# A recurrence's key norms taken by tokens and spread back by products, with new orders on three engines

## The reference

```python
kk = heads(k * p['k_k'])
kk = kk / jnp.maximum(jnp.sqrt(jnp.sum(kk * kk, axis=-1, keepdims=True)), 1e-12)
k = k * (1 + (a - 1) * p['k_a'])
decay = jnp.exp(-jnp.exp(heads(w)))
def step(S, inp):                      # b_t = kk_t * a_t
    sa = jnp.einsum('bhvk,bhk->bhv', S, kk_t)
    S = S * d_t[:, :, None, :] - sa[..., None] * b_t[:, :, None, :] + v_t[..., None] * k_t[:, :, None, :]
    return S, jnp.einsum('bhvk,bhk->bhv', S, r_t)
yn = ((y - mean) * lax.rsqrt(var + GN_EPS)).reshape(B, T, D) * p['lnx_g'] + p['lnx_b']
bonus = jnp.sum(heads(r * k * p['r_k']), -1, keepdims=True) * heads(v)
out = ((yn + bonus.reshape(B, T, D)).astype(h.dtype) * g) @ p['wo']
```

## Time and profile before

| | us |
|---|---|
| median of three timed runs | 3330.76 |
| the three runs | 3322.47, 3330.76, 3331.25 |
| the profiled execution | 3320.69 |
| its span in the trace | 3319.1 |
| TensorE busy, share of the span | 96% |
| VectorE busy, share of the span | 64% |
| ScalarE busy, share of the span | 42% |

### The profile page before, as it was taken

One profiled execution on the slowest core, in us unless ns is written; L12 is line 12 of the kernel. 1 busy time (PEld: TensorE's weight loads), 2 busy tenths in 40 slices (PEclk: granted clock), 3 DMA queues, 4 the chain that ended last, 5 costly groups with the idle time before them and its releaser, 6 DMA issues. The chain is left out here.

```text
span 3319.1 us, 80335 instructions
## 1 busy us (share of the span) xinstructions
PE 3188.2 (96%) x31492; PEld 2974.0 (90%) x31492; DVE 2127.6 (64%) x3654; ACT 1387.5 (42%) x2180; POOL 128.7 (4%) x245
## 2 busy tenths in 40 slices
PE   6999997888899999999999999999999999999998
PEld 3799986666799999999999988998999999999998
DVE  4544547778558778778778875555578855444455
ACT  2333325566345324334334564334455334343342
POOL 0000000000000000000000000000000000000000
PEclk9999999999999999999999999999999999999999
DMA  9877740000777888878867532342356754544443
GB/s 397 308 270 283 286 169 20 19 18 19 263 297 276 304 304 294 312 289 302 310 225 242 188 125 96 124 153 91 124 197 218 254 184 162 163 163 165 164 163 118
DMA packets 182917, 668.77 MB, mean 201 GB/s; under 512 B 21366, under 2 KB 21536, under 8 KB 182208
## 3 DMA queue, kind: packets, MB, share of 16 engines
q1 hardware_dynamic: 155808, 570.48, 48.2%
q0 software_dynamic: 26912, 95.47, 8.7%
HBM read 661.78 MB, written 4.09 MB: 201 GB/s over the span
## 5 line engine op out<-in xcount | busy, mean ns | idle before, releaser
L1127 DVE TENSOR_TENSOR sb_wlo<-sb_raw,sb_whi 128x1024 fp32r<-128x1024 f32 x778 | 942.8, 1222 | 523.5 <-ACT sb_whi L706 521.6
L706 ACT ACTIVATE sb_whi<-sb_raw 128x1024 fp32r<-128x1024 f32 x778 | 811.8, 1057 | 1107.9 <-PE ps L1941 1001.7
L1939 PE MATMUL ps<-sb_ah,sb_whi 128*128 128x288 f32 x3728 | 1111.1, 298 | 11.4 <-DVE sb_al L1333 6.9
L1940 PE MATMUL ps<-sb_ah,sb_wlo 128*128 128x288 f32 x3728 | 1099.7, 295 | 0.0
L1941 PE MATMUL ps<-sb_al,sb_whi 128*128 128x288 f32 x3728 | 1096.2, 294 | 0.0
L1939 PEld LDWEIGHTS ps<-sb_ah,sb_whi 128*128 128x128 f32 x3728 | 698.4, 187 | 38.5 <-issue 33.8
L1941 PEld LDWEIGHTS ps<-sb_al,sb_whi 128*128 128x128 f32 x3728 | 702.0, 188 | 0.0
L1940 PEld LDWEIGHTS ps<-sb_ah,sb_wlo 128*128 128x128 f32 x3728 | 699.9, 188 | 0.1
L1939 PE MATMUL ps<-sb_bh,sb_whi 128*128 128x288 f32 x2048 | 607.4, 297 | 0.0
L1940 PE MATMUL ps<-sb_bh,sb_wlo 128*128 128x288 f32 x2048 | 604.1, 295 | 0.0
L1941 PE MATMUL ps<-sb_bl,sb_whi 128*128 128x288 f32 x2048 | 602.2, 294 | 0.0
(11 more groups left out here) (307 smaller groups left out, 3346.0 us busy)
## 6 DMA issues: line engine op xcount, KB each, us to landing
sb_raw<-stream SPq DMA_DIRECT2D x1070, 512.0 KB, 4.5
sb_strip<-strips POOLq DMA_DIRECT2D x156, 512.0 KB, 5.0
sb_crow<-crow POOLq DMA_DIRECT2D x8, 512.0 KB, 5.4
sb_x<-xT SPq DMA_DIRECT2D x1, 2304.0 KB, 15.6
sb_x<-xT POOLq DMA_DIRECT2D x1, 2304.0 KB, 9.3
yT<-sb_x SPq DMA_DIRECT2D x4, 576.0 KB, 2.8
sb_lwa<-lw POOLq DMA_DIRECT2D x16, 130.0 KB, 2.3
sb_lwg<-lw POOLq DMA_DIRECT2D x16, 130.0 KB, 2.4
```

The source lines that it names most:

```text
L706: nc.scalar.activation(whi[:, q % SPL, :], raw[:, n, :], ACT.Copy).then_inc(hi_ready, 1)
L1127: nc.vector.tensor_tensor(wlo[:, q % SPL, :], raw[:, n, :], whi[:, q % SPL, :], ALU.subtract).then_inc(lo_ready, 1)
L1939: mm(out, wh, xh, start=start, stop=False)
L1940: mm(out, wl, xh, start=False, stop=False)
```

## The change

The vectors k_k and k_a are put at the end of the table `vec` (32 more columns) and leave the lane's weights; the three scalars made of them (k_k squared, minus k_k, 1 - k_a) are computed once for all 16 pairs ahead of the stage (`prm`, 3 x 16 columns), and `gain` keeps only its wait for the free lane. `ssq` is ten products of one column, which put the sum of squares of each token in a partition; `floor` and `norm` work on 5 columns (`kn`); a new `spread` on TensorE multiplies the inverses, broadcast along a row, with the identity, so that 320 columns lie in PSUM again, and `removal` reads them there behind a new wait. `normed` subtracts and scales with two operations over 320 columns in place of five tensor-scalars. `gated` is cut in `output` (the addition) and `gated` (the product with the gate), and TensorE's `grams` in `gram_b` and `gram_k`. The lists of the three engines are put in a new order; the places within a turn are to be seen in the diff. Semaphore counts follow.

```diff
@@ -61,7 +61,9 @@
...
-NVEC = QG + 4
+KKG = QG + 4
+KAG = KKG + KB
+NVEC = KAG + KB
...
@@ -73,16 +75,16 @@
...
-PW0, PA0, PKK, PKA = range(2 * P, 2 * P + 4)
+PW0, PA0 = range(2 * P, 2 * P + 2)
...
-Z, SSQ, NAT, GK, GB = range(1, 6)
+Z, SSQ, SPR, NAT, GB, GK = range(1, 7)
...
-BONUS, GATE, BACK = range(1, 4)
-PRE, INVY, INVT, TOKM, POST, MSK, CHN = 5, 5, 6, 5, 3, 2, 4
+BONUS, BACK, GATE = range(1, 4)
+PRE, INVY, INVT, TOKM, POST, MSK, CHN = 6, 5, 6, 5, 3, 2, 4
...
@@ -92,7 +94,7 @@
...
-FRONT_CHAIN, BACK_CHAIN = 8, 15
+FRONT_CHAIN, BACK_CHAIN = 5, 12
...
@@ -303,6 +305,7 @@
...
+        prm = sb("prm", [P, 3, KB], "SMALL", 736)
...
@@ -328,7 +331,7 @@
...
-                                + [("st", [P, 2, C]), ("bn", [P, NCH, 6]), ("ag", [P, NCH, 2]), ("rs", [P, 8]), ("prm", [P, 3])]):
+                                + [("st", [P, 2, C]), ("bn", [P, NCH, 6]), ("ag", [P, NCH, 2]), ("rs", [P, 8]), ("kn", [P, 8])]):
...
@@ -836,9 +839,8 @@
             def gains(u, it):
...
-                act.wait_ge(m["omk"], it + 1)
-                nc.scalar.activation(t["t5"][:], t["sa"][:], ACT.Identity, scale=t["lwa"][:, PKA:PKA + 1],
-                                     bias=t["prm"][:, 0:1]).then_inc(m["t5"], 1)
+                nc.scalar.activation(t["t5"][:], t["sa"][:], ACT.Identity, scale=vec[:, bass.ds(2 * it + (KAG + u), 1)],
+                                     bias=prm[:, 0, bass.ds(2 * it + u, 1)]).then_inc(m["t5"], 1)
...
@@ -892,37 +894,39 @@
                 t = lanes[0 if f is None else f]
                 if f is not None:
                     sigmoids(f, i)
-                    gains(f, i)
-                    token(f, i, T_V, t["vt"][:], "ps")
                 if g is not None:
                     products(g, j)
                 if f is not None:
+                    token(f, i, T_V, t["vt"][:], "ps")
                     decay(f, i, 0)
+                    gains(f, i)
+                if g is not None:
+                    state(g, j, 0, CH_0)
+                if f is not None:
                     decay(f, i, 1)
                 if g is not None:
-                    state(g, j, 0, CH_0)
                     state(g, j, 1, CH_14)
+                if f is not None:
+                    token(f, i, T_KK, t["km"][:, :, 0, :], "ps")
+                if g is not None:
                     state(g, j, 2, CH_2)
                     state(g, j, 3, CH_3)
                     state(g, j, 4, CH_3)
-                if f is not None:
-                    token(f, i, T_KK, t["km"][:, :, 0, :], "ps")
-                if g is not None:
                     root(g, j)
                 if f is not None:
                     inverse(f, i, 1)
+                    inverse(f, i, 2)
                     token(f, i, T_MV, t["km"][:, :, 1, :])
-                    inverse(f, i, 2)
+                if g is not None:
+                    back(g, j)
+                if f is not None:
                     inverse(f, i, 3)
                     token(f, i, T_B, t["ng"][:, :, 0, :])
                 if g is not None:
-                    back(g, j)
-                if f is not None:
-                    token(f, i, T_K, t["kt"][:])
-                    inverse(f, i, 4)
-                if g is not None:
                     high(g, j)
                 if f is not None:
+                    inverse(f, i, 4)
+                    token(f, i, T_K, t["kt"][:])
                     inverse(f, i, 5)
...
             def turn(it):
@@ -1444,6 +1448,10 @@
...
+            kk = vec[:, KKG:KKG + KB]
+            ch.inc(nc.vector.tensor_tensor(prm[:, 2, :], kk, kk, ALU.mult))
+            ch.inc(nc.vector.tensor_scalar(prm[:, 1, :], kk, -1.0, None, ALU.mult))
+            ch.inc(nc.vector.tensor_scalar(prm[:, 0, :], vec[:, KAG:KAG + KB], -1.0, 1.0, ALU.mult, ALU.add))
...
@@ -1470,27 +1478,22 @@
             def gain(u, it):
...
-                dve.wait_ge(m["lwa"], 16 * it + 16)
-                kk = t["lwa"][:, PKK:PKK + 1]
-                ch.inc(tt(t["prm"][:, 2:3], kk, kk, ALU.mult))
-                ch.inc(nc.vector.tensor_scalar(t["prm"][:, 1:2], kk, -1.0, None, ALU.mult))
-                nc.vector.tensor_scalar(t["prm"][:, 0:1], t["lwa"][:, PKA:PKA + 1], -1.0, 1.0, ALU.mult, ALU.add).then_inc(m["omk"], 1)
...
             def squares(u, it):
...
-                stt(out=t["n2"][:], in0=kb, scalar=t["prm"][:, 2:3], in1=kb, op0=ALU.mult, op1=ALU.mult).then_inc(m["sq"], 1)
+                stt(out=t["n2"][:], in0=kb, scalar=prm[:, 2, bass.ds(2 * it + u, 1)], in1=kb, op0=ALU.mult, op1=ALU.mult).then_inc(m["sq"], 1)
...
             def floor(u, it):
...
-                ch.inc(nc.vector.tensor_scalar(t["n2"][:], t["ps"][:, Z_K:Z_K + TT], 1e-24, None, ALU.max))
+                ch.inc(nc.vector.tensor_scalar(t["kn"][:, 0:NCH], t["ps"][:, Z_K:Z_K + NCH], 1e-24, None, ALU.max))
...
             def norm(u, it):
...
-                ch.inc(nc.vector.reciprocal(t["n2"][:], t["n2"][:]))
+                nc.vector.reciprocal(t["kn"][:, 0:NCH], t["kn"][:, 0:NCH]).then_inc(m["sq"], 1)
...
@@ -1502,28 +1505,29 @@
...
-                be, kk = flat(t["bE"][:]), t["lwa"][:, PKK:PKK + 1]
+                be, kk = flat(t["bE"][:]), vec[:, bass.ds(2 * it + (KKG + u), 1)]
...
+            def erased(u, it):
+                t, m = lanes[u], L[u]
+                kb = flat(k[:, bass.ds(2 * it + u, 1), :])
+                dve.wait_ge(m["ex"], 2 * it + 1)
+                stt(out=t["kr"][:, :, 0, :], in0=chunks(kb), scalar=prm[:, 1, bass.ds(2 * it + u, 1)], in1=t["e"][:, :, 0:C],
+                    op0=ALU.mult, op1=ALU.mult).then_inc(m["prep"], 1)
+
             def received(u, it):
...
-                dve.wait_ge(m["ex"], 2 * it + 1)
...
-            def erased(u, it):
-                t, m = lanes[u], L[u]
-                kb = flat(k[:, bass.ds(2 * it + u, 1), :])
-                stt(out=t["kr"][:, :, 0, :], in0=chunks(kb), scalar=t["prm"][:, 1:2], in1=t["e"][:, :, 0:C],
-                    op0=ALU.mult, op1=ALU.mult).then_inc(m["prep"], 1)
-
             def removal(u, it):
...
+                dve.wait_ge(m["pre_mm"], PRE * it + SPR)
...
-                ch.inc(tt(be, be, t["n2"][:], ALU.mult))
+                ch.inc(tt(be, be, t["ps"][:, Z_K:Z_K + TT], ALU.mult))
...
@@ -1598,24 +1602,24 @@
...
-                for c in range(NCH):
-                    ins = nc.vector.tensor_scalar(t["yn"][:, c, :], t["ps"][:, Z_Y + C * c:Z_Y + C * c + C], t["ag"][:, c, 0:1],
-                                                  t["rs"][:, c:c + 1], ALU.subtract, ALU.mult)
-                    if c < NCH - 1:
-                        ch.inc(ins)
-                    else:
-                        ins.then_inc(m["yn"], 1)
+                ch.inc(tt(t["yn"][:], chunks(t["ps"][:, Z_Y:Z_Y + TT]), t["ag"][:, :, 0:1].to_broadcast([P, NCH, C]), ALU.subtract))
+                ch.wait()
+                tt(t["yn"][:], t["yn"][:], t["rs"][:, 0:NCH].rearrange("p (c t) -> p c t", t=1).to_broadcast([P, NCH, C]),
+                   ALU.mult).then_inc(m["yn"], 1)
...
             def bonus(u, it):
...
-            def gated(u, it):
+            def output(u, it):
...
+
+            def gated(u, it):
+                t, m = lanes[u], L[u]
...
@@ -1636,37 +1640,36 @@
                     squares(f, i)
                 if g is not None:
                     level(g, j, 5)
-                    bonus_in(g, j)
+                    solved(g, j)
                 if f is not None:
                     floor(f, i)
                 if g is not None:
-                    solved(g, j)
+                    products(g, j)
                 if f is not None:
+                    removed(f, i)
+                    running(f, i)
                     norm(f, i)
                 if g is not None:
-                    products(g, j)
-                if f is not None:
-                    running(f, i)
-                    removed(f, i)
-                if g is not None:
+                    bonus_in(g, j)
                     carries(g, j)
                 if f is not None:
+                    erased(f, i)
                     received(f, i)
-                    erased(f, i)
                     removal(f, i)
                     insertion(f, i)
+                    level(f, i, 0)
                 if g is not None:
                     moments(g, j)
                 if f is not None:
-                    level(f, i, 0)
                     grams(f, i)
                     level(f, i, 1)
                 if g is not None:
-                    bonus(g, j)
+                    normed(g, j)
                 if f is not None:
                     level(f, i, 2)
                 if g is not None:
-                    normed(g, j)
+                    bonus(g, j)
+                    output(g, j)
                 if f is not None:
                     level(f, i, 3)
                 if g is not None:
@@ -2127,20 +2130,32 @@
...
             def ssq(u, it):
...
-                pe.wait_ge(m["sq"], it + 1)
```

(66 more changed lines are left out.)

2 lines of the change are left out of this document (1 added, 1 removed).

## The result

The changed kernel takes 3290.61 us (median of four runs, 3289.40 to 3291.39), the kernel before on the same chip 3326.61 us (3320.52 to 3331.25): ratio 0.9896, 95% interval 0.9883 to 0.9909, a gain of 36 us where 43 were forecast. The span of the profiled execution went from 3319.1 to 3287.9 us, 31.2 less. The difference of the two gaps lies in the kernel before: its runs spread over 11 us and the profiled one is at their lower end, while those of the changed kernel lie within 2 us. (A ratio here is estimated from all runs of a group and is not quite the quotient of the two medians; both lie in the interval.) Further runs of the changed kernel gave 3290.23 and 3289.84 us (ratio 0.9897 both times), beside 3328.54 and 3323.78 us for the kernel before.

A forecast was written before the change was run, and what follows sets the result against it. Bound: a chain passing between engines, repeated each turn of the recurrence. 1.65 + 0.1 + 0.9 = 2.67 us a turn (3.07 behind the loop's jump) gave 43 us: 3320.7 to 3278, median 3283, range 3264 to 3312.

The forecast's parts named there:

- the 5 us that were added for the distance between profiled execution and median: Expected median 3283 us, 5 us above the profiled execution's forecast of 3278 us.
- Part 1: Turn's start to the carries: reciprocal off the path, carries at 4.1 instead of 5.76, gain 1.65 us (1.2 to 1.8).
- Rival (a): New orders worth nothing, only the reciprocal leaves the path: 16 us gained, 3305 to 3315 us; chance 0.22.
- Part 2: Carries to level 0, with the new spread: 7.7 instead of 7.84, gain 0.1 us (0.4 to a loss of 0.8).
- slack of the round trip: Between carries and level 0: small reciprocal done at 5.2, sums before the spread at 6.5, 1.3 us of slack.
- Part 3: Level 0 to the next turn: 7.66 instead of 8.57, gain 0.9 us (0.2 to 1.4).
- After the stage everything moves up as it is: Behind the recurrence: later work only starts earlier, as hardly any transfers run in the stage; no size given.
- (b): The norm's round trip between engines replaces the reciprocal on the path: no change, 3321 to 3331 us; chance 0.07.
- (c): Granted clock falls in the recurrence: slower from about 3 low turns on, 3355 us at 5; chance 0.07 with other slowing.
- (d): Spread hides wholly and TensorE's waits shrink more: 3.6 us in a turn, 3260 to 3266 us; chance 0.04.

The follow-up runs named there:

- orders alone: Changed kernel with the old norm over 320 columns (wide reciprocal, no spread), new orders, scalars and two-operation scaling kept: 3318.91 us, ratio 0.9984.
- norm alone: Kernel before with the new norm by tokens (narrow reciprocal, spread), its orders, lane scalars and five tensor-scalars kept: 3309.50 us, ratio 0.9954.
- tokens-v ahead: Changed kernel with tokens-v ahead of the products again in TensorE's and ScalarE's queues: 3296.77 us, ratio 0.9922.
- late norm: Changed kernel with the small reciprocal moved behind bonus-in, two additions and the erased keys in VectorE's queue: 3295.88 us, ratio 0.9919.
- old tail: Changed kernel with the order of before from level 1 on, on all three engines, two-operation scaling kept: 3304.64 us, ratio 0.9935.
- five tensor-scalars: Changed kernel with five tensor-scalars back in place of the two operations over 320 columns: 3295.08 us, ratio 0.9912.
- fetch moved: Changed kernel with the load of the next low-rank weights issued at a turn's start instead of 11 us into it: 3291.24 us, ratio 0.9889.

## Why the prediction was right, and what it missed

The time was hit more closely than the gain. In the trace 43 us were forecast and 31.2 came; of the 5 us that were added for the distance between profiled execution and median 1.2 came (3290.61 against 3289.40). The one error covers a third of the other, and that is luck.

**Part 1** (5.76 to 4.1): 4.14, and the time is right, but the cause only in part. The orders alone bring the carries to 4.17, with the wide reciprocal moved behind the copy; the norm alone brings them to 4.72, and with tokens-v ahead the changed kernel has 4.71. So the early carries come from the order, and what the narrow reciprocal is needed for lies in part 2: kept wide, it stands ahead of the gains, and level 0 comes 1.9 us later. Rival (a), in which the reciprocal by itself gave 1.65 here, gets 1.04.

**Part 2** (7.84 to 7.7): 7.71. The slack of the round trip was 1.27 us against 1.3, and the late norm shows that it isn't more. The spread is hidden better than forecast: 0.3 of its 0.58 were to be hidden, and the norm alone shows 0.07 paid. TensorE needs 2.96 us from the carries to state 1 before and 3.05 now, for the recall and the wait for ScalarE's scaled copy that stood there are gone. The removal starts 0.21 behind state 1, which follows the spread, and about 0.1 later than its queue would let it.

**Part 3** (8.57 to 7.66): 7.89, so 0.68 us where 0.9 were forecast. By the old tail and the five tensor-scalars the order gives about 0.4 of it and the two wide operations 0.24 of their 0.35.

**The mis-sized term** is this part, and it stands in the part's end. Up to level 2 the layout was right within 0.05 us; then gate (15.80 against 15.7) and level 3 (17.37 against 17.2) slip by 0.1 to 0.2, and from level 4 to the next turn there are 0.85 us (690.28 to 691.13) where I had 0.7, although show 1.01 for the same step (686.23 to 687.24). A turn of 19.70 instead of 19.5 is 15 x 0.2 = 3 us. The new groups cost 0.61 (sums of squares) and 0.68 us (spread), a little over the 0.58 that I took from one distance of the earlier trace rows. The Trainium skill (TensorEngine Tiling, Instruction Overhead) has one column cost what some sixty do: the trace agrees, 0.61 us for ten products of one column, and 0.58 to 0.68 for ten of 64 columns.

**The missing term** is the stops. Fifteen undisturbed turns would have given 15 x (22.33 - 19.70) = 39.5 us, 3.5 less than forecast; the stops and the clock (with the 0.8 of the jump) took 8.3 - 3.1 = 5.2 of it back in the fourteen full turns and 0.9 more went in the fifteenth. With 0.1 in the filling turn, 0.9 in the drain and 1.2 elsewhere (0.3 were forecast) this is the way from 43 to 31.2. That the waits of 1.6 and 1.2 us in each turn of the kernel before covered most of such stops is argued from their absence there; no run shows it by itself. In the drain I had put nothing: back waits for VectorE, and the gate behind it runs at half the clock. TensorE of the changed kernel in the drain:

```profile
825.45 0.90 PE L2098 MATMUL ps<-sb_con,sb_yt 64*64 64x64 f32 x20 [1.69 <-DVE sb_yt L1607]
826.27 1.33 PE L2268 MATMUL ps<-sb_mids,sb_lwg 128*128 128x288 f32 x2
```

The gate's two products take 1.33 us instead of 0.75 behind that wait, and the granted clock of the stretch is 0.83 where it was 0.91. "After the stage everything moves up as it is" held but for the 1.2 us; that the drain would be as before, which the sum took without saying it, did not.

**The rivals.** (a) falls by the old tail and tokens-v, together 1.5 us in a turn. (b) is real and 1.3 us away. (c) didn't decide: one turn in fifteen of the changed kernel has a clock of 0.93, and the kernel before has two. But its mechanism is in the orders alone, where every second turn falls to 0.92, and it is cheaper than the 14 us a turn that I priced, because the clock is low for a part of the turn only: about 0.85 us there, 1.5 and 1.8 in the two low turns of the kernel before, 3.9 in the one of the norm alone. Two figures of (c) were wrong from the start. By its own terms five low turns lose 5 x 14 and the ten others gain 10 x 2.9, so the kernel would be 41 us slower, not 27; and the earlier trace rows leave 8.6 us of idle time in 50, that is 3.8 us in a turn of 22.2, not 6, with 18.3 us of work and not 16.8. (d) had both the hidden spread and shorter waits; the spread does hide nearly whole, but the turn is 19.70 us, where (d) wanted 18.6.

## What to carry over

A chain that passes between engines and repeats is best priced by laying one turn out, queue by queue, with the durations of the trace, from meeting place to meeting place; that hit the carries and level 0 here within 0.05 us and the turn within 0.2, while the busy shares said nothing. A second thing can be late close behind the first: a change that removes one of them alone gives little (14 and 5 us here) and must not be judged before both are gone (36 us). A time that comes out right does not show its cause: the early carries were put down to the reciprocal, and the order makes them. Doubling a group prices the next one, not the first. Price a new group by the range of start-to-start distances of its form, not by one of them, and keep a term for what the removed waits had covered.

## What the hardware showed unexpectedly

TensorE, with small products issued densely, stops now and then for 0.2 to 1.75 us with nothing to wait for, mostly at places bound to its program: ten times in the changed stage of 345 us, in every fourth turn at nearly the same place, and in other turns once 32 products had been put ahead.

The granted clock didn't fall by how busy TensorE was on average (18.48 of 19.70 us at 1.00), but behind idle stretches, and not behind all: with a wait of 1.36 us in every turn every second turn fell to 0.92, the others stayed at 1.00; a stop of 1.75 us was followed by 0.93 over its turn, while one of 1.52 us in the same stretch of a turn, with the fetch moved, left it at 1.00 (18.91 of 22.31 us busy):

```profile
629.02 0.46 PE L2100 MATMUL ps<-sb_yt,sb_p 64*64 64x64 f32 x17 [1.52 <-issue]
```

In the run with the old tail one turn of 23.0 us fell to 0.85 behind a stop of 0.68 and a wait of 0.62 close together:

```profile
655.71 0.33 PE L2106 MATMUL ps<-sb_yt,sb_p 64*64 64x64 f32 x3 [0.68 <-issue]
...
656.66 0.56 PE L2106 MATMUL ps<-sb_p,sb_yt 64*64 64x64 f32 x20 [0.62 <-ACT sb_yt L856]
...
659.13 1.33 PE L2098 MATMUL ps<-sb_yt,sb_p 64*64 64x64 f32 x20
```

The last group takes 1.33 us where it takes 0.80 at full clock. A product of 64 rows by one column costs no less than one by 64 columns in these groups, and a reciprocal takes 2.13 us for 320 columns and 0.16 for five.
